# A second accumulator for the modulation sums, LayerNorm scaling between later splits, and attention's modulation one stage ahead

## The chip, the cores and the metric

The kernel runs on one core of a Trainium2 chip. The metric is the device time of one execution in microseconds: 3281.18 us, the median of three runs (3276.89 to 3293.57).

## What is computed

Two transformer blocks of two layers each, in float32, on 256 tokens of 1024 features. Each sublayer is steered by a modulation: a row of 9216 numbers, `silu(cond) @ w_mod + b_mod`, cut into shift, scale and gate for each of three sublayers. The first block has two streams (latent and context), each with a condition of its own.

```python
def modulation(cond, w_mod, b_mod):
    m = jax.nn.silu(cond) @ w_mod + b_mod
    return jnp.split(m[..., None, :], N_MOD, axis=-1)

def ffn_sublayer(x, shift, scale, gate, w_in, w_out, ln_g, ln_b):
    y = swiglu(modulate(x, shift, scale), w_in, w_out)
    return layer_norm(ALPHA * x + 0.5 * gate * y, ln_g, ln_b)
...
        x_lat = ffn_sublayer(x_lat, m_lat[0], m_lat[1], m_lat[2], ...)
        x_ctx = ffn_sublayer(x_ctx, m_ctx[0], m_ctx[1], m_ctx[2], ...)
        h_lat = modulate(x_lat, m_lat[3], m_lat[4])
        # gMLP in layer 0, grouped-query attention in layer 1, here y_lat, y_ctx
        x_lat = layer_norm(ALPHA * x_lat + m_lat[5] * y_lat, ln_g[i, 1], ln_b[i, 1])
        x_lat = ffn_sublayer(x_lat, m_lat[6], m_lat[7], m_lat[8], ...)
```

The second block has RMS norms, a mixer and one stream. The change doesn't touch its code.

## The kernel before

The program is a list of twelve stages, `subs`, numbered by `s["i"]`: 0 ffn, 1 gMLP, 2 ffn, 3 ffn, 4 attention, 5 ffn (first block), 6 to 11 the second block. Stages 0 to 3 work on both streams (512 tokens wide), stage 5 on one (256). Attention takes in both and gives out one. All five engines run one hand-written instruction stream each, and semaphores tie them together.

**Units.** Weights come in units of 1 MB, by SyncE, into two buffers `wraw`. ScalarE copies a unit to a rounded high half `wh` (L816), VectorE subtracts to get the low half `wl` (L1200, `split_next`), and TensorE makes three matmuls for each product (high-high, low-high, high-low). `split_next(u)` splits unit u + 1. The buffer of a unit is free to be split again when TensorE is done with the unit before, so a split stands on the way from one unit to the next but one.

**An ffn stage of two streams** has two groups, of 12 and of 10 units of `w_in`, each followed by an output phase of 6 or 5 units of `w_out`. A `w_in` unit is 48 matmuls (L2137) into a pair of PSUM banks. ScalarE takes silu of one half (L914), VectorE multiplies it with the other (L1580, "the product"), which frees the pair (`pair_free`), and GpSimd splits the result (L660, L661). The first two units of a stage are done stream by stream in `begin_two`, and `gate_rows` (L2067) follows them. Stage 0 has its gate rows after unit 2, since its gate is summed in the stage itself. Stage 5 has one group of 22 units.

**Modulation.** Each stage computes the modulation of the next one, `nxt`, in three sections (shift, scale, gate) of four pieces. A piece (`mod_unit`) is a 1 MB load into one of two buffers `mraw` and two accumulations for each condition (L1173, 128x1024) into `acc`. So a piece is four instructions with two streams and two with one. `acc` holds a sum that is still spread over the 128 partitions. For shift and scale TensorE sums it to columns, by matmuls with a vector of ones (`column` between the matmuls of a unit, L2056, or `columns` in one block, L2047). VectorE copies these out of PSUM (`mod_end`, L1193). For the gate `gate_rows` does the summing. There is one `acc`, so section 1 can begin only when section 0's columns are read. Tables give the unit at which each piece is summed (`TWO_MODS`), loaded (`TWO_LOADS`) and turned into columns (`TWO_COLUMNS`). They have one row for stage 0 (`True`) and one for stages 1 to 3. The order in VectorE's queue in unit i is: split, pieces, product, `mod_end`. Where the columns are in unit i, the first piece of a section comes after them (`late_mods`).

In attention (stage 4) all twelve pieces for stage 5 are spread by hand between the steps for keys, queries and heads, with `columns(nxt, 0, 7)` before unit 5 and `columns(nxt, 1, 6, 480)` at head 5.

**LayerNorm.** `layer_norm` leaves x without gain and bias. The next stage applies them in `scale_x` (L1316, four full-width operations for each stream), in its first output phase. `load_ln` on GpSimd's queue brings gain and bias to `lnp` (L675), in the stage before the one that uses them. VectorE lets it go on by `ln_used`.

**Queues.** SyncE issues all weight and modulation loads in one order. A piece's load waits until the piece two before it has been summed (`mod_used`), and all that stands behind it waits too. GpSimd issues the loads of gains.

Of the kernel before, what the change touches and what calls it, by code (L numbers as in the profile page):

```python
# [6 lines left out]
P = 128  # L7
# [38 lines left out]
ATT_LOADS = (1, 1, 5, 5, 7, 7, 8, 8, 9, 9, 9, 9)  # L46
# [132 lines left out]
def program(nc, ins, out, subs):  # L179
    u_end = subs[-1]["n_unit"] + dict(ffn=33, gmlp=36, attn=10, mix=16)[subs[-1]["kind"]]  # L180
    with ExitStack() as ctx:
# [247 lines left out]
        def early_mods(s, idx):  # L429

            return [(sec, q) for sec, q in two_mods(s, idx) if q or two_columns(s, idx) is None]

        def late_mods(s, idx):

            return [(sec, q) for sec, q in two_mods(s, idx) if not q and two_columns(s, idx) is not None]
# [44 lines left out]
        def _(sp):  # L480
# [83 lines left out]
            for s in subs:  # L564
# [15 lines left out]
                elif s["kind"] == "ffn":  # L580
                    m0 = 0
                    for g, n in enumerate(s["groups"]):

                        halves = lambda idx: [w_in[:, :, t, bass.ds(idx + m0, 1), :].rearrange("p k m c -> p k (m c)") for t in range(2)]
                        if two(s) and g == 0:
                            first_phase(s, n, halves, nxt, True)
                        else:
                            phase(n, 2 if g else 8, halves, None if g else nxt, by_column=True)
# [13 lines left out]
                elif s["kind"] == "attn":  # L602
# [8 lines left out]
                    for idx in range(10):  # L611
# [6 lines left out]
                        for n, at in enumerate(ATT_LOADS):  # L618
                            if at == idx:
                                load_mod(nxt, n // 4, n % 4, n // 4 * 4 + (12 * nxt["i"] + n % 4 + 1))  # L620
# [22 lines left out]
        def _(pool):  # L643
# [27 lines left out]
            def load_ln(s):  # L671

                pool.wait_ge(ln_used, s["i"])
# [39 lines left out]
            for s in subs:  # L713
# [30 lines left out]
                elif s["kind"] == "ffn":  # L744
                    m0 = 0
                    for g, n in enumerate(s["groups"]):
# [3 lines left out]
                        if g == 0 and s["i"] < B2 - 1:  # L750
                            load_ln(s)
# [18 lines left out]
                elif s["kind"] == "attn":  # L770
                    power(nrm1[:, 16:24], 8)
                    for u in range(4):
                        power(nrm1[:, 4 * u:4 * u + 4], 4)
                    load_ln(s)
# [32 lines left out]
        def _(act):  # L807
# [69 lines left out]
            for s in subs:  # L877
# [270 lines left out]
        def _(dve):  # L1148
# [11 lines left out]
            def mod_unit(s, sec, q):  # L1160
# [9 lines left out]
                for jj in range(2):  # L1170
                    for c in cs:
                        v = 2 if s["block"] == 2 else c
                        op = dve.scalar_tensor_tensor(out=acc[:, c], in0=mraw[:, q % 2, jj],  # L1173
                                                      scalar=svec[:, v, 2 * q + jj:2 * q + jj + 1],
                                                      in1=biasrow[:] if q == jj == 0 else acc[:, c],
# [326 lines left out]
            for s in subs:  # L1502
# [64 lines left out]
                elif s["kind"] == "ffn":  # L1567
# [3 lines left out]
                    for g, n in enumerate(s["groups"]):  # L1571
# [10 lines left out]
                        if two(s) and g == 0:  # L1582
                            for i in range(n):
# [7 lines left out]
                                for sec, q in early_mods(s, i):  # L1591
# [4 lines left out]
                                elif s["i"] == 0 and i == 2:  # L1596
# [1199 lines left out]
```

## Time and profile before

| | before |
|---|---|
| median of 3 runs | 3281.18 us (3276.89 to 3293.57) |
| profiled execution | 3288.56 us |
| its span | 3286.8 us |
| mean granted TensorE clock | 0.971 |
| instructions | 46905 |

The profile is of one execution. Where an instruction had to wait, its row has in brackets the idle time of the engine before it and who ended that. Stages in this execution, by the starts of their first units: 0 from about 50 us, 1 from 450, 2 from 920, 3 from 1330, 4 from 1735, 5 from 1903, the second block from 2112. The granted clock is a share of 2.4 GHz. A matmul's end is modelled, so neighbours overlap in the rows, and start-to-start times or windows are the safer measure.

### The profile page before, as it was taken

How to read it: one execution, taken by the hardware profiler on the slowest of the kernel's cores; microseconds unless marked ns; L12 is line 12 of the kernel's file. 1: busy time of each engine (PE TensorE's matmuls, PEld its weight loads, DVE VectorE, ACT ScalarE, POOL GpSimd, SP SyncE). 2: the span in 40 equal slices, each digit the busy share in tenths (PEclk: the TensorE clock that was granted, in tenths of full speed). 3: DMA queues.
4: the chain of work that ended last, by engine and by line, in shares of the span. 5: the costliest groups of instructions: out<-in, count | busy, mean ns of one | idle time of the engine just before them, and what ended most of it. 6: DMA issues, size and time to landing. Idle time of an engine off the chain costs nothing.

```text
span 3286.8 us, 46905 instructions
## 1 busy us (share of the span) xinstructions
PE 3116.7 (95%) x19332; PEld 2765.7 (84%) x19332; DVE 2028.1 (62%) x2134; ACT 986.5 (30%) x1027; POOL 688.1 (21%) x640
## 2 busy tenths in 40 slices
PE   8889999999998999989998899999989999999899
PEld 5668889978887888878887698899888999988899
DVE  4653357667366643765437777576687767667764
ACT  2111222212121112212113455333533334353433
POOL 1120110024112111121100011131371304228110
PEclk9989999999999999999999999999899999999999
DMA  7443335322235332443333477496546869754464
GB/s 250 151 156 94 98 90 181 128 90 77 91 114 167 133 97 90 125 153 133 90 118 118 165 218 246 161 269 229 179 167 179 269 207 263 244 183 151 149 184 155
DMA packets 501663, 522.73 MB, mean 159 GB/s; under 512 B 15732, under 2 KB 433830, under 8 KB 501478
## 3 DMA queue, kind: packets, MB, share of 16 engines
q1 hardware_dynamic: 498536, 513.76, 48.6%
q0 software_dynamic: 2944, 6.32, 0.9%
q8 instruction: 140, 2.29, 0.3%
q14 instruction: 43, 0.35, 0.0%
HBM read 518.97 MB, written 1.05 MB: 158 GB/s over the span
## 4 chain that ended last, share of the span: by engine, by line
PE 77%; DVE 13%; POOL 3%; issue 3%; ACT 3%; DMA 2%; SPq 0%; ACTq 0%; DVEq 0%; POOLq 0%
PE ps L2137 22%; PE ps L2311 15%; PE ps L2223 14%; PE ps L2335 7%; DVE acc L1173 5%; PE ps L2165 5%; DVE wl L1200 3%; PE ps L2202 2%; POOL wst L786 1%; PE ps L2181 1%; ACT wh L816 1%; PE ps L2047 1%; POOL lnp L792 1%; DMA mraw<-in_w_mod 1%; PE ps L2249 1%
## 5 line engine op out<-in xcount | busy, mean ns | idle before, releaser
L1200 DVE TENSOR_TENSOR wl<-wraw,wh 128x2048 fp32r<-128x2048 f32 x341 | 832.4, 2441 | 602.9 <-ACT wh L816 597.4
L816 ACT ACTIVATE wh<-wraw 128x2048 fp32r<-128x2048 f32 x341 | 652.7, 1914 | 952.1 <-PE ps L2223 406.7
L2137 PE MATMUL ps<-xh,wh 128*128 128x512 f32 (+1 forms) x1504 | 567.5, 377 | 7.1 <-DVE wl L1200 6.4
L2137 PE MATMUL ps<-xl,wh 128*128 128x512 f32 (+1 forms) x1504 | 554.7, 369 | 0.0
L2137 PE MATMUL ps<-xh,wl 128*128 128x512 f32 (+1 forms) x1504 | 553.9, 368 | 0.0
L1173 DVE SCALAR_TENSOR_TENSOR acc<-mraw,svec,acc 128x1024 f32<-128x1024 f32 x329 | 438.0, 1354 | 27.1 <-DMA mraw<-in_w_mod 11.0
L660 POOL CAST hh<-ht 128x256 f32 (+1 forms) x176 | 146.0, 830 | 1267.4 <-DVE ht L1580 934.1
L2311 PE MATMUL ps<-xh,wh 128*128 128x258 f32 x1408 | 403.4, 287 | 5.3 <-DVE xl L1398 4.4
L2311 PE MATMUL ps<-xh,wl 128*128 128x258 f32 x1408 | 399.5, 284 | 0.0
L2311 PE MATMUL ps<-xl,wh 128*128 128x258 f32 x1408 | 399.2, 284 | 0.0
L2137 PEld LDWEIGHTS ps<-xh,wh 128*128 128x128 f32 x1504 | 285.3, 190 | 54.9 <-issue 6.6
L2137 PEld LDWEIGHTS ps<-xl,wh 128*128 128x128 f32 x1504 | 284.8, 189 | 49.5
L2137 PEld LDWEIGHTS ps<-xh,wl 128*128 128x128 f32 x1504 | 285.3, 190 | 45.3 <-issue 0.7
L2311 PEld LDWEIGHTS ps<-xh,wh 128*128 128x128 f32 x1408 | 268.4, 191 | 10.2 <-DVE xl L1398 7.6
L2165 PE MATMUL ps<-wh,xh 128*128 128x256 f32 x832 | 247.7, 298 | 24.8 <-DVE wl L1200 24.8
L2311 PEld LDWEIGHTS ps<-xl,wh 128*128 128x128 f32 x1408 | 268.9, 191 | 0.0
L2311 PEld LDWEIGHTS ps<-xh,wl 128*128 128x128 f32 x1408 | 268.5, 191 | 0.0
L914 ACT ACTIVATE sg<-ps 128x512 f32<-128x512 f32 (+1 forms) x88 | 48.0, 546 | 653.4 <-PE ps L2137 620.0
L2165 PE MATMUL ps<-wl,xh 128*128 128x256 f32 x832 | 240.8, 289 | 0.0
L2165 PE MATMUL ps<-wh,xl 128*128 128x256 f32 x832 | 240.6, 289 | 0.0
L1580 DVE TENSOR_TENSOR ht<-ps,sg 128x512 f32<-128x512 f32 (+1 forms) x88 | 54.8, 623 | 291.7 <-ACT sg L914 291.7
L2223 PE MATMUL ps<-wh,hh 128*128 128x512 f32 x520 | 207.2, 398 | 10.1 <-DVE wl L1200 7.6
(423 smaller groups left out, 5658.0 us busy)
## 6 DMA issues: line engine op xcount, KB each, us to landing
wraw<-in_ffn_w_in SPq DMA_DIRECT2D x352, 512.0 KB, 5.1
wraw<-in_ffn_w_out SPq DMA_DIRECT2D x176, 512.0 KB, 4.2
mraw<-in_ada_w SPq DMA_DIRECT2D x72, 1024.0 KB, 7.0
mraw<-in_w_mod SPq DMA_DIRECT2D x64, 1024.0 KB, 6.8
wraw<-in_gmlp_w_in SPq DMA_DIRECT2D x48, 512.0 KB, 4.5
wraw<-in_mix_w_in SPq DMA_DIRECT2D x48, 512.0 KB, 4.7
wraw<-in_gmlp_w_out SPq DMA_DIRECT2D x24, 512.0 KB, 4.1
first_w<-in_w_mod SPq DMA_DIRECT2D x8, 1024.0 KB, 11.6
```

The lines of the kernel that those rows point to most:

```text
L660: steps.link(pool.tensor_copy(hh[:, where], ht[:, par, 0:width]))
L816: act.activation(wh[:, slot], wraw[:, slot], ACT.Copy).then_inc(whi_done, 1)
L914: act.activation(sg[:, pair, 0:W], ps[:, 2 * pair, 0:W], ACT.Silu).then_inc(sg_ready, 1)
L1173: op = dve.scalar_tensor_tensor(out=acc[:, c], in0=mraw[:, q % 2, jj], scalar=svec[:, v, 2 * q + jj:2 * q + jj + 1], in1=biasrow[:] if q = ...
L1200: dve.tensor_tensor(wl[:, slot], wraw[:, slot], wh[:, slot].bitcast(F32), ALU.subtract)\
L1580: dve.tensor_tensor(ht[:, pair, 0:W], ps[:, 2 * pair + 1, 0:W], sg[:, pair, 0:W], ALU.mult)\
L2137: m = pe.matmul(ps[:, bank, 0:width], a, b, start=k == p == 0, stop=k == KD - 1 and p == 2)
L2165: m = pe.matmul(to, a, b, start=k == p == 0, stop=k == KD - 1 and p == 2)
L2202: m = pe.matmul(ps[:, 2 * t + half], a, b, start=False, stop=i == kk == 1 and p == 2, skip_group_check=i == 0)
L2223: m = pe.matmul(ps[:, bank0 + 2 * t + half], a, b, start=start and kk == p == 0, stop=stop and kk == 1 and p == 2, skip_group_check=not st ...
L2311: m = pe.matmul(ps[:, 2 * pair + r, 0:XW], a, b, start=n == p == 0, stop=n == KD - 1 and p == 2)
L2335: m = pe.matmul(ps[:, j, 0:T], a, b, start=i == kk == p == 0, stop=i == KF // 2 - 1 and kk == 1 and p == 2, skip_group_check=i == 5)
```

## The change

- Section 1 of the modulation is summed into `lnp` in stages 0 to 3 (function `summed`), and `TWO_COLUMNS` moves the columns later: in stage 0 from units 6 and 9 to 7 and 10, in the others from 5 and 8 to 6 and 10. `early_mods` and `late_mods` go. All pieces of a unit come ahead of its product.
- `load_ln` moves into the stage that uses what it loads. It waits for section 1's columns.
- In two-stream stages `scale_x` is called for one stream at a time, after the second and the third split of the output phase and not before them all. In the gMLP the same.
- Stage 0's gate rows go from unit 2 to unit 3.
- Sections 0 and 1 for stage 5 leave attention for the second group of stage 3, two pieces in each of the units 2 to 5 (`NEXT_MODS`), with columns in units 5 and 7. They are summed in the two halves of `lnp`. Attention keeps section 2, at heads 1, 3, 5 and 6. For this, stage 3's second group is written out where it was a loop on VectorE, SyncE and TensorE.
- ScalarE's first group of stage 5 is written out too (`if g == 0`).

```diff
-ATT_LOADS = (1, 1, 5, 5, 7, 7, 8, 8, 9, 9, 9, 9)
+ATT_MODS, ATT_LOADS = (1, 3, 5, 6), (5, 5, 9, 9)
-TWO_MODS = {True: (3, 4, 4, 5, 6, 7, 8, 8, 9, 10, 11, 11), False: (2, 3, 3, 4, 5, 6, 7, 7, 8, 9, 10, 11)}
-TWO_LOADS = {True: (5, 6, 7, 7, 8, 9, 10, 10, 11, 11, 12, 12), False: (3, 4, 5, 6, 7, 8, 9, 9, 10, 11, 11, 12)}
-TWO_COLUMNS = {True: (6, 9), False: (5, 8)}
+TWO_MODS = {True: (4, 4, 5, 5, 6, 7, 7, 8, 9, 10, 10, 11), False: (2, 3, 3, 4, 5, 6, 7, 7, 8, 9, 10, 11)}
+TWO_LOADS = {True: (5, 6, 7, 7, 8, 9, 9, 10, 11, 11, 12, 12), False: (3, 4, 5, 6, 7, 8, 9, 9, 10, 11, 11, 12)}
+TWO_COLUMNS = {True: (7, 10), False: (6, 10)}
+NEXT_MODS, NEXT_LOADS, NEXT_COLUMNS = (2, 2, 3, 3, 4, 4, 5, 5), (3, 3, 5, 5, 6, 6, 7, 7), (5, 7)
...
+        def summed(s, sec, c):
+
+            if s["i"] == 5 and sec in (0, 1):
+                return lnp[:, sec]
+            return lnp[:, c] if 0 < s["i"] < 5 and sec == 1 else acc[:, c]
...
-            def load_ln(s):
-
-                pool.wait_ge(ln_used, s["i"])
+            def load_ln(at):
+
+                pool.wait_ge(ln_used, at["i"] - 1)
+                if at["i"] < 5:
+                    pool.wait_ge(mcol_done, sections(subs[5 if at["i"] == 4 else at["i"] + 1], 1) + 1)
+                s = subs[at["i"] - 1]
...
-                        if two(s) and g == 0:
+                        if g == 0:
                             for i in range(n):
-                                if i:
+                                if i or not two(s):
                                     split_next(u0 + i)
                                 evac(i, i % 2, 0)
...
-                                for sec, q in early_mods(s, i):
+                                for sec, q in two_mods(s, i):
                                     mod_unit(nxt, sec, q)
                                 evac(i, i % 2, 0)
...
-                                for sec, q in late_mods(s, i):
-                                    mod_unit(nxt, sec, q)
+                        elif s["i"] == 3:
+                            for i in range(n):
+                                split_next(u0 + i)
+                                for sec, q in ahead(s, i, NEXT_MODS):
+                                    mod_unit(subs[5], sec, q)
+                                evac(i, i % 2, 0)
+                                if ahead_columns(s, i) is not None:
+                                    mod_end(subs[5], ahead_columns(s, i))
...
-                        if g == 0:
+                        if one:
                             scale_x(s, s["post"])
-                            if unscaled(s):
-                                dve.sem_inc(ln_used, 1)
...
+                        if two(s) and g == 0:
+                            for i in range(n // 2 - 1):
+                                split_next(u0 + n + 1 + i)
+                                if 0 < i < 3:
+                                    scale_x(s, (i - 1,))
```

## Rows read from the trace of the kernel before

**Rows 1.** Page, section 1: busy us, share of the span, number of instructions
```profile
PE 3116.7 (95%) x19332; PEld 2765.7 (84%) x19332; DVE 2028.1 (62%) x2134; ACT 986.5 (30%) x1027; POOL 688.1 (21%) x640
```

**Rows 2.** Waits of TensorE: total us, times, longest
```profile
PE ps L2056 <- DVE acc L1173: 35.4, 8, 6.5
PE ps L2165 <- DVE wl L1200: 24.8, 9, 5.6
PE ps L2223 <- DVE wl L1200: 15.1, 4, 7.1
```

**Rows 3.** TensorE's timeline, stages 2 and 1: start, us, [idle before, releaser]
```profile
1004.32 0.38 PE L2056 MATMUL ps<-ones,acc 128*128 128x1 f32 x2 [2.25 <-DVE acc L1173]
...
1047.80 0.59 PE L2056 MATMUL ps<-ones,acc 128*128 128x1 f32 x2 [6.51 <-DVE acc L1173]
...
700.86 0.79 PE L2223 MATMUL ps<-wh,gm_h 128*128 128x512 f32 x1 [7.10 <-DVE wl L1200]
```

**Rows 4.** ScalarE's timeline: activations that end a unit, stages 0, 1, 2
```profile
103.87 0.60 ACT L914 ACTIVATE sg<-ps 128x512 f32<-128x512 f32 x1 [17.19 <-PE ps L2137]
...
150.50 0.60 ACT L914 ACTIVATE sg<-ps 128x512 f32<-128x512 f32 x1 [22.25 <-PE ps L2137]
...
196.04 0.60 ACT L914 ACTIVATE sg<-ps 128x512 f32<-128x512 f32 x1 [20.95 <-PE ps L2137]
...
550.75 1.09 ACT L932 ACTIVATE v<-ps 128x512 f32<-128x512 f32 x2 [13.08 <-PE ps L2165]
...
595.99 1.09 ACT L932 ACTIVATE v<-ps 128x512 f32<-128x512 f32 x2 [19.74 <-PE ps L2165]
...
1001.41 0.60 ACT L914 ACTIVATE sg<-ps 128x512 f32<-128x512 f32 x1 [8.59 <-PE ps L2137]
...
1018.43 0.60 ACT L914 ACTIVATE sg<-ps 128x512 f32<-128x512 f32 x1 [14.62 <-PE ps L2137]
...
1065.10 0.60 ACT L914 ACTIVATE sg<-ps 128x512 f32<-128x512 f32 x1 [22.07 <-PE ps L2137]
```

**Rows 5.** VectorE's timeline in stage 2, ahead of section 0's columns
```profile
981.87 3.28 DVE L1200 TENSOR_TENSOR wl<-wraw,wh 128x2048 fp32r<-128x2048 f32 x1 [1.11 <-ACT wh L816]
985.07 10.08 DVE L1173 SCALAR_TENSOR_TENSOR acc<-mraw,svec,acc 128x1024 f32<-128x1024 f32 x8
...
997.87 6.39 DVE L1173 SCALAR_TENSOR_TENSOR acc<-mraw,svec,acc 128x1024 f32<-128x1024 f32 x4
```

**Rows 6.** TensorE's timeline: the gate rows of stage 2
```profile
964.80 3.60 PE L2067 MATMUL ps<-acc,ones 128*128 128x512 f32 x8
```

**Rows 7.** Windows: stretch, its us, TensorE busy (instructions), PEclk, DMA share, GB/s
```profile
218.22:298.01 79.79, 71.30 (x288) 56.66 (x288) 0.94 0.35 116
682.32:737.32 55.00, 47.90 (x192) 37.75 (x192) 0.91 0.30 96
1098.10:1165.47 67.37, 67.36 (x288) 53.67 (x287) 1.00 0.34 110
...
700.00:704.00 4.00, 3.14 (x7) 0.50 0.98 258
```

**Rows 8.** Attention: window of L1173 on VectorE, and TensorE's column blocks
```profile
1753.93:1903.39 149.46, 30.77 (x24) 0.92 0.44 145
...
1808.48 3.57 PE L2047 MATMUL ps<-ones,acc 128*128 128x1 f32 x16 [4.69 <-DVE acc L1173]
...
1855.38 1.84 PE L2047 MATMUL ps<-ones,acc 128*128 128x1 f32 x16
```

**Rows 9.** Stage 5: a table load on ScalarE, and TensorE's waits for splits
```profile
1933.70 1.28 ACT L914 ACT_TABLE_LOAD   x1 [2.77 <-PE ps L2137]
...
PE ps L2137 <- DVE wl L1200: 4.9, 8, 1.2
```

**Rows 10.** DMA issues: queue, number, size, median us from issue to landing
```profile
mraw<-in_w_mod SPq DMA_DIRECT2D x64, 1024.0 KB, 6.8
...
lnp<-in_ln_b POOLq DMA_DIRECT2D x5, 512.0 KB, 5.8
```

More of the change, by code:

```diff
@@ L427, in two_columns, with ahead, ahead_columns @@
             return at.index(idx) if idx in at else None
[L429 to L435, printed above, removed]
+        def ahead(s, idx, table):
+            return [(n // 4, n % 4) for n, at in enumerate(table) if at == idx] if s["i"] == 3 else []
+        def ahead_columns(s, idx):
+            return NEXT_COLUMNS.index(idx) if s["i"] == 3 and idx in NEXT_COLUMNS else None
+        def summed(s, sec, c):
+            if s["i"] == 5 and sec in (0, 1):
+                return lnp[:, sec]
+            return lnp[:, c] if 0 < s["i"] < 5 and sec == 1 else acc[:, c]
         def two(s):
@@ L586, in _ @@
                             first_phase(s, n, halves, nxt, True)
+                        elif s["i"] == 3:
+                            for idx in range(n):
+                                load(unit[0] + idx, unit[0] + idx, halves(idx), True)
+                                for sec, q in ahead(s, idx, NEXT_LOADS):
+                                    load_mod(subs[5], sec, q, sec * 4 + (12 * 5 + q + 1))
+                            unit[0] += n
                         else:
@@ L1611, in _ @@
                         last = g == 1 and two(s)
-                        phase(n // 2 - (2 if last else 1), u0 + n + 1, 2)
+                        if two(s) and g == 0:
[3 more added lines that the diff above has]
+                                    scale_x(s, (i - 1,))
+                        else:
+                            phase(n // 2 - (2 if last else 1), u0 + n + 1, 2)
+                        if g == 0 and unscaled(s):
+                            dve.sem_inc(ln_used, 1)
                         u0 += n + n // 2
@@ L1699, in _ @@
                             split_next(u1 + i)
+                            if g == 0 and 0 < i < 3:
+                                scale_x(s, (i - 1,))
+                        if g == 0:
+                            dve.sem_inc(ln_used, 1)
                         u1 += n
@@ L1712, in stage, with unit @@
                         AV.wait(dve, name, 0)
-                    def unit(i, taken=()):
+                    def unit(i):
                         split_next(u0 + i)
-                        for n in taken:
-                            mod_unit(nxt, n // 4, n % 4)
                     def sums(name, squares, to):
@@ L2363, in _ @@
                                 m.then_inc(w_used, 1)
-                                if s["i"] == 0 and i == 2:
+                                if s["i"] == 0 and i == 3:
                                     gate_rows(s)
+                        elif s["i"] == 3:
+                            pe.wait_ge(y_half, s["n_half"] + g)
+                            for i in range(n):
+                                pe.wait_ge(wlo_done, u0 + i + 2)
+                                pe.wait_ge(pair_free, s["n_inq"] + m0 + i)
+                                sec = ahead_columns(s, i)
+                                for r in range(2):
+                                    m = features((u0 + i) % 2, 2 * ((s["n_inq"] + m0 + i) % 2) + r, r, slice(0, W), W, False,
+                                                 None if sec is None else lambda n: column(subs[5], sec, n))
+                                m.then_inc(w_used, 1)
                         else:
@@ L2531, in _ @@
                             scores(h + 2)
-                        if h == 5:
-                            AV.wait(pe, "lo_3", 0)
-                            columns(nxt, 1, 6, 480)
                         if h == 7:
```

58 lines of the change are left out of this document (23 added, 35 removed).

## The prediction

> **What bounds the kernel now.** I read the engine table of the page first. TensorE is busy for 3116.7 of 3286.8 us and VectorE for 2028.1 [rows 1]. So TensorE sets the time, and only two things can be won: the 170 us in which it stands, and work on it that is slower than it need be. The table of waits of TensorE says who makes it stand [rows 2]. First comes L2056 behind L1173, 35.4 us in 8 waits: `column` turns the summed modulation row into columns and finds the sum unfinished. Then come weight splits (L1200) that arrive late, 24.8 and 15.1 us. Single waits stand in TensorE's timeline [rows 3]: 2.25 us at 1004.32 and 6.51 at 1047.80 in stage 2, 7.10 at 700.86 in the gMLP.
>
> A wait costs more than itself. I measure that on ScalarE, whose activation waits for the end of each unit: its idle time grows by just what a unit is longer. A plain unit leaves it idle for 8.59 us. The unit with section 0's columns leaves 14.62, and the one with section 1's leaves 22.07 [rows 4]. The first is 6.03 over, of which the wait is 2.25 and the sixteen columns are the rest, 3.8 us. The second is 13.5 over: 6.51 wait, 3.8 columns, and 3.2 that neither explains. The windows of the output phases show what that is: the same 288 matmuls take 67.37 us at granted clock 1.00 in stage 2 and 79.79 at 0.94 in stage 0; 192 of them take 55.00 at 0.91 in the gMLP [rows 7]. After the gMLP's wait of 7.10 us the granted clock is 0.50, which is 1.2 GHz of 2.4, in the first 4 us [rows 7]. So I price each place by the lengthened unit or phase and not by the wait.
>
> **The columns and the second accumulator (stages 0 to 3).** Why is the sum late? VectorE's queue has a unit's split, its modulation pieces, then the product that frees PSUM. Two pieces are 10.08 us, so one is 5.0, and once 6.39 [rows 5]. Between them, from 995.15 to 997.87, stand a product and a split, 2.7 us; a split alone can take 3.28 [rows 5]. So a unit with two pieces is 12.8 us of VectorE or more, against 11.2 of TensorE (67.37 / 6) [rows 7]. In stage 2 the last piece of section 0 ends at 997.87 + 6.39 = 1004.26; TensorE was ready for it 2.25 us before 1004.32. The change puts those columns one unit (11 us) later, so the margin is 8 to 9 us. It also lets section 1 begin before they are read, in `lnp`, so the pieces are spread and not squeezed behind the columns. Section 1's columns go from unit 8 to unit 10. I walk the queue on from 1004.26 in stage 2 with these prices: TensorE ends unit 5 at 1012, unit 6 with the columns at 1027, and then a unit every 11. VectorE ends the product and the split of unit 6 at 1007, the first piece of section 1 at 1013, the second at 1023 (behind the product of unit 5 and a split), and the last two at 1043 (behind the product of unit 6 and a split). TensorE wants them at 1060, 17 us later, and every split ends 3 us or more ahead of its unit. In stage 0 the same walk leaves 5 us for section 0 and 12 for section 1. New pieces there are no more than before; only their order differs. What goes:
> - Stage 2: 14.62 − 8.59 − 3.8 = 2.2, and 22.07 − 8.59 − 3.8 = 9.7. Together 11.9. Stage 3 repeats the pattern to 0.3 us: 11.7.
> - gMLP (stage 1): of its two units with columns one has no wait and leaves 13.08, the other 19.74 [rows 4], so 6.7 goes.
> - Stage 0: 22.25 − 8.59 − 3.8 = 9.9, and 20.95 − 8.59 − 3.8 = 8.6. Its gate rows move behind unit 3. The unit that holds them leaves 17.19, 8.6 over; undisturbed gate rows cost 3.6 [rows 6], so 5.0 goes.
> - Stage 0's first output phase is 12.4 us longer than stage 2's [rows 7]. Its weights were late because SyncE's queue held the last modulation loads ahead of them, and these waited for pieces that stood behind the column wait. With the pieces earlier, the walk has the weights split about 2 us before TensorE asks. Gone: 12.4; what is late next is the last product, and it has the phase's two first tiles as cover.
>
> **LayerNorm scaling.** In the gMLP eight full-width operations stood in VectorE's queue ahead of two splits; TensorE waited 7.10 us [rows 3] and then ran slow. 192 matmuls at stage 2's pace are 44.9 us, and they took 55.0 [rows 7]: 10.1 goes. In the ffn stages there is no wait at this place, so the interleaving wins nothing there. Price: scaling now needs gain and bias that are loaded in the same stage, after the columns of section 1. The GpSimd queue issues that load behind its last split of hidden units. It lands after 5.8 us [rows 10]. Scaling starts after the second or third output unit is split, some 11 us on. Covered by one output unit; without that cover VectorE would stand with the next split behind it. The row speaks of loads that VectorE's splits ran beside as well.
>
> The Trainium skill, SBUF — State Buffer, section "SBUF: two separate sides", speaks against this move: a DMA issued by GpSimd needs it to write descriptors, and VectorE operations that hold the shared port keep it from that. [...]
>
> **Attention's modulation.** The stage has 24 accumulation instructions, 30.8 us of VectorE [rows 8], and VectorE is what its TensorE waits on. Sixteen of them (20.5 us), both column blocks and eight loads leave it; eight with two spaced loads stay. On TensorE itself goes: the 4.69 us wait, 3.57 and 1.84 us of columns, together 10.1 [rows 8]. That is the lower end. The upper is 20.5 + 5.4 = 25.9, if every instruction stood on the path. Following the query chain (sum, factor by GpSimd, turn, transposes, exponentials): the four pieces before the column wait hide partly behind waits for weights and for the factor, and from head 1 on TensorE's own work binds. I get 11 to 12.5 at each head, and take 12. The bounds I keep are 6 (another wait in its place) and 20.
> In stage 3's second group sixteen instructions, eight loads and two column blocks arrive. VectorE there: a split and a product, up to 4 us, and two one-stream pieces, four instructions of 30.77 / 24 us, 5.1: some 9 of 11.2 us. The splits stand ahead of the pieces. A 1 MB load lands in 6.8 us [rows 10], and a buffer turns round in 11.2. That is tight but ahead of need by one unit. Columns: eight in place of sixteen, 1.9 each time, −3.8.
>
> **Stage 5, a side effect.** ScalarE's loop over its 22 units is written out now. In the loop each turn of two units reloads the activation table twice, 1.28 us each [rows 9], between TensorE's end of a unit and the next split. TensorE waits 4.9 us there in 8 waits [rows 9]. Written out, one load is left. DMA is busy in this stage, so I take 3.5 (bounds 0 and 4.9). The wait at its output phase stays, since `one` keeps the scaling ahead of the split.
>
> The Trainium skill, ScalarE activation tables: per-element evaluation and per-set limits, section "Table sets in the compiler and the runtime", says that table loads are placed per block; that would be why the loop has them.
>
> **Sum.** Stage 0: 5.0 + 9.9 + 8.6 + 12.4 = 35.9. gMLP: 6.7 + 10.1 = 16.8. Stage 2: 11.9. Stage 3: 11.7 − 3.8 = 7.9. Attention 12. Stage 5 3.5. Together 88.0 us. The profiled execution took 3288.56 us (span 3286.8), the median of the runs is 3281.18, so 7.4 lower. 3288.6 − 88.0 = 3200.6; against the median 3193.2. I forecast 3193.
>
> **Rivals.** About 0.5% (16 us) is what a measurement of this kernel can tell from no change.
> 1. The moved pieces collide. In stage 3 each unit draws two 1 MB loads beside its weights, in one SyncE queue. If a load waits on a piece, the weights behind it come late, as in stage 0's output phase: that price is 12.4. Attention then gives 6. 88.0 − 12.4 − 6 = 69.6: 3212. For it: that very mechanism in rows 7. Against it: SyncE stands a unit ahead here. Chance 0.17.
> 2. Waits shrink but do not vanish. If VectorE is later than my walk by more than the 5 us of stage 0, TensorE still waits there and the slow stretches stay. Then stages 0 and 1 give half (26) and the others a third less (10): 52, 3229. For it: a piece of 5.0 us can take 6.39 [rows 5]. Chance 0.12.
> 3. The change does not do what it says: the queue of VectorE is as long as before, and TensorE waits for splits in place of sums. Left are attention and stage 5, 15: 3266. Against it: a unit with one piece needs 7.7 to 9.7 of 11.2 us. Chance 0.04.
> 4. Slower. The late LayerNorm load. If it lands later than about 14 us after its issue, VectorE stands in `scale_x`, the next split waits behind it, and TensorE too, in stages 1, 2 and 3. It decides against the whole change only from (88 + 16) / 3 = 35 us beyond that. At a landing of 50 us: 3 × 36 = 108 lost, 3301. The rows show 5.8. Chance 0.03.
> 5. More is won: attention gives 20 and stage 5 all of it, and stage 3's written-out group costs nothing for columns: 3181. Chance 0.06.
>
> **How the numbers follow.** The forecast has 0.58. The range takes in case 5 with its neighbourhood, case 1 and the faster part of case 2: 3174 to 3228. Faster by over 0.5% is everything but case 4 and most of case 3, which lies at the bound: 0.94. Within 0.5%: 0.03. Slower: 0.03.
>
> **What the new profile would show.** No wait of TensorE on the modulation sums in stages 0 to 3, and no idle time over about 13 us in front of an activation there (8.6 + 3.8). Stage 0's first output phase at 67 to 69 us; the gMLP's at 45. Attention's TensorE stretch, 149 us long, at 137 or so, with no L2047 work. Two or fewer table loads in stage 5. Eight-column blocks in stage 3's second group with no wait ahead of them. The forecast is wrong if waits for L1200 take the place of those for L1173, if VectorE waits for the gains in `scale_x`, or if weights come late from SyncE in stage 3.

## The result and the profile after

| | before | after |
|---|---|---|
| median (runs) | 3281.51 us (4) | 3187.11 us (4, 3177.8 to 3188.18) |
| ratio, 95% interval | | 0.9701 (0.9669 to 0.9732) |
| profiled execution, span | 3288.56, 3286.8 us | 3186.64, 3184.9 us |
| mean granted TensorE clock | 0.971 | 0.985 |
| instructions | 46905 | 46705 |

The forecast was 3193 us in a range of 3174 to 3228. The engine table of the page, against [rows 1]: TensorE is 37.0 us less busy, although it makes as many matmuls, and its idle time falls from 170 to 105 us.

```profile
PE   3079.7 (97%) x19332; PEld 2738.2 (86%) x19332; DVE 2031.3 (64%) x2134; ACT 958.2 (30%) x1006; POOL 693.3 (22%) x640
```

The table of TensorE's waits up to 2110 us (us in total, times, longest), against [rows 2], which count the whole program. Of the 24.8 us in their second row only 4.0 lie before 2110 us. The rest is in the second block, which the change leaves as it is. No wait on a modulation sum (now L1192) is left, and none on a split (L1219) is over 1.3 us. Attention's are the largest that remain of those that the change comes near. The first fence is of the kernel before, the second of the kernel after.

```profile
PE ps L2165 <- DVE wl L1200: 4.0, 3, 2.2
```
```profile
PE ps L2532 <- ACT ptb L1038: 6.9, 4, 3.3
PE ps L2491 <- DVE ql L1764: 6.8, 2, 4.9
...
PE ps L2185 <- DVE wl L1219: 1.8, 2, 0.9
PE ps L2243 <- DVE wl L1219: 1.7, 2, 1.3
```

VectorE's and TensorE's timelines in stage 2, against [rows 3, 5]. The sum of section 0 is ready at 939.19 + 6.39 = 945.6, and its columns begin at 954.20: 8.6 us to spare. Section 1's is ready at 983.9, its columns begin at 1001.88: 18 us.

```profile
939.19 6.39 DVE L1192 SCALAR_TENSOR_TENSOR acc<-mraw,svec,acc 128x1024 f32<-128x1024 f32 x4
...
973.83 10.09 DVE L1192 SCALAR_TENSOR_TENSOR lnp<-mraw,svec,lnp 128x1024 f32<-128x1024 f32 x8
...
954.20 0.28 PE L2076 MATMUL ps<-ones,acc 128*128 128x1 f32 x2
...
1001.88 0.28 PE L2076 MATMUL ps<-ones,lnp 128*128 128x1 f32 x2
```

ScalarE's activations that end those two units, against [rows 4]. Idle time was 14.62 and 22.07 us and is 12.1, a plain unit's 8.58 and the columns' 3.5.

```profile
953.71 0.60 ACT L932 ACTIVATE sg<-ps 128x512 f32<-128x512 f32 x1 [8.58 <-PE ps L2157]
968.20 0.60 ACT L932 ACTIVATE sg<-ps 128x512 f32<-128x512 f32 x1 [12.09 <-PE ps L2157]
...
1015.88 0.60 ACT L932 ACTIVATE sg<-ps 128x512 f32<-128x512 f32 x1 [12.08 <-PE ps L2157]
```

Windows of the first output phases of stage 0, the gMLP and stage 2, each from its first matmul, against [rows 7]. The columns here are the busy time of TensorE, its weight loads, VectorE, ScalarE and GpSimd, each with its number of instructions, then the granted clock, the DMA share and GB/s. All three run at clock 1.00. Stage 0's 79.79 us are 67.37, and the gMLP's 55.00 are 45.04.

```profile
189.99:257.36 67.37, 67.37 (x290) 54.04 (x289) 23.10 (x15) 11.97 (x7) 3.77 (x2) 1.00 0.33 104
633.18:678.22 45.04, 45.04 (x196) 36.24 (x195) 28.43 (x26) 6.68 (x4) 7.16 (x6) 1.00 0.36 117
1026.90:1094.27 67.37, 67.37 (x290) 54.03 (x289) 31.12 (x21) 11.96 (x7) 2.96 (x4) 1.00 0.36 110
```

I cut both profiled executions at the same events (first activation of a stage, first matmul of attention's end, second unit of stage 5's output phase) and compare the pieces:

| piece | forecast | gained |
|---|---|---|
| before stage 0's first activation (67.11 and 63.73) | 0 | 3.4 |
| stage 0 | 35.9 | 35.1 |
| gMLP | 16.8 | 20.2 |
| stage 2 | 11.9 | 12.1 |
| stage 3 | 7.9 | 9.4 |
| attention | 12 | 14.9 |
| stage 5 | 3.5 | 7.0 |
| second block | 0 | −0.1 |
| sum | 88.0 | 101.9 |

### The profile page after: what moved, and what is told of

The parts are those of the page before. It is cut to its first block, busy times and chain, and to the rows that moved or that the text cites. A ratio compares the mean times of both kernels' runs of the same rounds, so it can differ in the third digit from the quotient of the medians.

```text
span 3184.9 us, 46705 instructions
## 1 busy us (share of the span) xinstructions
PE 3079.7 (97%) x19332; PEld 2738.2 (86%) x19332; DVE 2031.3 (64%) x2134; ACT 958.2 (30%) x1006; POOL 693.3 (22%) x640
## 4 chain that ended last, share of the span: by engine, by line
PE 85%; DVE 8%; POOL 3%; ACT 2%; issue 1%; DMA 1%; SPq 0%; DVEq 0%; ACTq 0%; POOLq 0%
PE ps L2157 29%; PE ps L2331 15%; PE ps L2243 15%; PE ps L2355 8%; PE ps L2185 6%; PE ps L2222 2%; DVE wl L1219 2%; POOL wst L804 1%; PE ps L2201 1%; POOL lnp L810 1%; PE ps L2269 1%; PE ps L2065 1%; PE ps L2628 1%; ACT wh L834 1%; PE ps L2094 1%
## 5 line engine op out<-in xcount | busy, mean ns | idle before, releaser
L1219 DVE TENSOR_TENSOR wl<-wraw,wh 128x2048 fp32r<-128x2048 f32 x341 | 835.0, 2449 | 586.3 <-ACT wh L834 580.9
L1192 DVE SCALAR_TENSOR_TENSOR acc<-mraw,svec,acc 128x1024 f32<-128x1024 f32 x259 | 343.0, 1344 | 15.4 <-DMA mraw<-in_ada_w 10.2
L674 POOL TENSOR_TENSOR hl<-ht,hh 128x256 f32 (+1 forms) x176 | 219.2, 1246 | 29.2 <-POOL hh L673 29.2
```

What stands on the lines that cost most here:

```text
L674: pool.tensor_tensor(hl[:, where], ht[:, par, 0:width], hh[:, where].bitcast(F32), ALU.subtract)\
L1192: op = dve.scalar_tensor_tensor(out=to, in0=mraw[:, q % 2, jj], scalar=svec[:, v, 2 * q + jj:2 * q + jj + 1], in1=biasrow[:] if q == jj == ...
L1219: dve.tensor_tensor(wl[:, slot], wraw[:, slot], wh[:, slot].bitcast(F32), ALU.subtract)\
```

## Experiments

Each was timed against the kernel before on its own chip. Ratios are to be read beside the 0.9701 of the kernel after. Because a single execution scatters by several us, places are compared in the traces. How much it scatters shows behind stage 5's last silu: from there to the end, where only the faster version below changes anything, the 14 profiled executions take 1240 to 1250 us. Stage 0, the largest piece, has no experiment of its own: its 35.1 us rest on the comparison of the two traces.

### The later columns, or the second accumulator?

```diff
-TWO_COLUMNS = {True: (7, 10), False: (6, 10)}
+TWO_COLUMNS = {True: (7, 10), False: (5, 8)}
```

> The kernel after, with TWO_COLUMNS for stages 1 to 3 back at units 5 and 8; the second accumulator stays, and all pieces stay ahead of their product. It parts the two halves of that edit. Theory A, the later columns do the work: the sums stand as late as before, each of the six column units waits, about 2 us for section 0 and 6 us with a slow stretch for section 1, and the 30 us of stages 1 to 3 come back. Theory B, the single accumulator was the cause, since section 1 could only start behind section 0's columns: with the second one in place section 0 waits 2.2 us as before, section 1 no more than that, 13 us at most come back. Theory C, both are slack by now: 0.

Measured: 3219.30 us, ratio 0.9792 (0.9762 to 0.9822), 32 us slower than the kernel after by the medians and 30 by the ratios. In the trace the stretches from stage 0 to 2, from 2 to 3 and from 3 to 5 are each 10.1 to 10.4 us longer, 30.6 in all: theory A in its total. Its single waits were sized wrongly. TensorE's waits of that kernel:

```profile
PE ps L2076 <- DVE lnp L1192: 12.3, 3, 4.1
...
PE ps L2076 <- DVE acc L1192: 6.1, 3, 2.3
```

Section 1 waits 4.1 us in stages 2 and 3 and not 6.5, so the second accumulator alone does take waiting away, 2.4 us in each. But section 0's short waits are now followed by slow stretches: in stage 3 it waits 2.24 us, then the granted clock is 0.50 for 4 us, and the unit is 20.15 us long where before it was 17.00 with the same wait.

```profile
1357.00:1361.00 4.00, 4.00 (x13) 3.42 (x14) 4.00 (x3) 0.00 (x0) 3.16 (x2) 0.50 0.32 123
```

By the lengths of their units the columns gained 33.5 us in these stages (8.7, 12.5 and 12.3), and 30.6 go when the positions go back. The second accumulator seems to make room for the later positions, since section 1 need no longer start behind section 0's columns. That is argued and not shown: no run has the later columns with one accumulator.

### LayerNorm scaling alone

```diff
-                        if g == 0:
-                            scale_x(s, s["post"])
-                            if unscaled(s):
-                                dve.sem_inc(ln_used, 1)
-                        elif unscaled(nxt):
+                        if g and unscaled(nxt):
                             factors(nxt)
                         for i in range(n - g):
                             split_next(u1 + i)
+                            if g == 0 and 0 < i < 3:
+                                scale_x(s, (i - 1,))
+                        if g == 0:
+                            dve.sem_inc(ln_used, 1)
```

> The kernel before, with one part of the change: in the gMLP the LayerNorm scaling is called stream by stream behind the second and third split of the output phase. Theory A, the forecast's: the wait of 7.10 us goes, and with it the slow stretch behind it, so the 192 matmuls of that output phase take 45 us in place of 55.0: 10 us faster. Rival B: only the wait goes, the clock has fallen for another reason: 7 us. Rival C: the splits now stand behind the four operations of each stream and are late in turn: 0 to 3 us.

Measured: 3278.18 us (10 runs), ratio 0.9981 (0.9965 to 0.9997), so 1 to 11 us faster. The window of the output phase, from its first matmul to its end, is 45.04 us at clock 1.00, where [rows 7] has 55.00 at 0.91. That is theory A: 10.0 us, of which 7.10 were the wait. The median shows 7 of them; two column units of the same stage were 3.7 us longer in this execution, with nothing changed there.

```profile
684.86:729.90 45.04, 45.04 (x196) 36.24 (x195) 28.42 (x26) 6.69 (x4) 7.22 (x6) 1.00 0.37 117
```

### Does idling lower the clock?

`keep_going` is a helper that the kernel before has already: matmuls on constants whose result nobody reads.

```diff
                 if n == 0:
+                    if sec == 1:
+                        keep_going(7, 44)
                     pe.wait_ge(mod_used, sec * 4 + (12 * s["i"] + 6))
```

> The kernel before, with 44 matmuls of 128x128 on constants (0.117 us each, 5.15 us, from the row of 32 in 3.74 us) put ahead of TensorE's wait for section 1's sum in stages 0 to 3. The waits there are 6.51, 5.25, 6.51 and 6.50 us and TensorE has nothing else to do, so the useful work begins no earlier. Theory A, standing idle is what lowers the clock: the granted clock is 1.00 behind the wait and not 0.50, and each of the four units is 2.3 to 3.5 us shorter (8.85, 7.7, 10.0 and 9.7 over an undisturbed one, less the wait): 11 us faster than the kernel before. Rival B, the clock falls for another reason (the loads that come in just then, or the column matmuls): no change.

Measured: 3287.85 us, ratio 1.0004 (0.9993 to 1.0014). Not a verdict for B: I had mispriced the filler. In the trace each of its matmuls is two records. TensorE's row for it in stage 2:

```profile
1039.03 9.98 PE L2076 MATMUL ps<-ident,ones 128*128 128x128 f32 x88
```

The wait of 6.51 us has become 9.98 us of work, and still the unit ends as early as before (24.32 us after the one before it, against 24.47). In the gMLP and in stage 0 the filled unit is longer, by 2.1 and 0.7 us. What follows the filler runs at clock 1.00 in all four places, where before the same place has 0.50 (windows in stage 2, first of the kernel with the filler, second of the kernel before). The DMA share, the number before the last, speaks against incoming loads as the cause: it is 1.08 in the first window, at clock 1.00, and 0.00 in the second, at 0.50.

```profile
1050.00:1054.00 4.00, 4.00 (x23) 3.42 (x23) 0.00 (x0) 0.00 (x0) 0.37 (x1) 1.00 1.08 312
```
```profile
1047.80:1051.20 3.40, 3.40 (x10) 2.92 (x11) 2.75 (x2) 0.00 (x0) 2.51 (x2) 0.50 0.00 0
```

So I halved it (`keep_going(7, 22)`).

> The kernel before, with 22 filling matmuls ahead of the wait for section 1's sum, where the run with 44 had too many: there each is two records, 88 records took 9.98 us in stage 2, longer than the wait of 6.51, and the granted clock stayed 1.00. 22 take 5.0 us and fit in the wait. Theory A (idling lowers the clock, and the slow stretch costs useful time): clock 1.00 behind the wait, about 1.5 us of wait left, and the units of section 1 are 21 us in stages 2 and 3 in place of 24.47 and 24.23, in all four 9 to 11 us less. Theory B: the units keep their length, since what follows the wait is slow for another reason (columns that read a sum just written, loads coming in).

Measured: 3274.01 us, ratio 0.9956 (0.9939 to 0.9973), 9 to 20 us faster than the kernel before, with matmuls added that compute nothing. In stage 3 the filler takes 5.07 us, 1.59 of wait are left, the granted clock behind it is 1.00, and the unit is 21.26 us and not 24.23.

```profile
1450.38 0.38 PE L2058 MATMUL ps<-ones,acc 128*128 128x1 f32 x2 [1.59 <-DVE acc L1173]
```
```profile
1450.40:1454.40 4.00, 4.00 (x23) 3.48 (x24) 2.73 (x2) 0.00 (x0) 3.13 (x2) 1.00 0.02 5
```

Theory A holds where the wait was filled wholly: the slow stretch comes from standing idle, not from the loads or the columns. With half the filler it isn't sure at each place: in stages 0 and 2 of this run the clock behind the remaining 1.59 us was 0.63, and these units are only 0.5 and 1.6 us shorter. The four filled units are 7.0 us shorter together, less than the 9 to 11 expected, and section 0's units of the gMLP and stage 2, which have no filler, are 0.9 and 3.1 longer. Of the 11.1 us between the two profiled executions 7.6 lie behind stage 5's last silu, where nothing was changed. So the four runs are faster, but the traces account for only a part of it.

### Attention

```diff
-ATT_MODS, ATT_LOADS = (1, 3, 5, 6), (5, 5, 9, 9)
+ATT_LOADS = (1, 1, 5, 5, 7, 7, 8, 8, 9, 9, 9, 9)
...
                     queries(0)
+                    mod_unit(nxt, 0, 1)
...
-                        if h in ATT_MODS:
-                            mod_unit(nxt, 2, ATT_MODS.index(h))
+                        if h < 4:
+                            mod_unit(nxt, 1, h)
+                        elif h > 4:
+                            mod_unit(nxt, 2, h - 5)
```

with the remaining pieces and both column blocks back likewise, and none of it in stage 3.

> The kernel after, with the modulation of sections 0 and 1 for stage 5 back in attention (all twelve pieces, both column blocks, the old loads) and out of stage 3's second group. Theory A, the forecast's: attention is longer by its 12 (bounds 6 to 20), stage 3 shorter by 3.8 for eight columns twice: +8. Theory B, by the landmarks of the two traces: attention +14.9, stage 3 -3.8 (units 12.87 against 11.0), so +11. Rival: attention's gain came from entering it in a better state (no slow stretch, weights ahead) and not from the pieces: then it stays within 5 us of the kernel after.

Measured: 3197.18 us, ratio 0.9730 (0.9704 to 0.9755), 10 us slower than the kernel after. The windows from the first matmul of stage 3's last output phase to the first of stage 5, of the kernels before, after and this one (columns as in [rows 7], TensorE's, its weight loads', VectorE's, ScalarE's and GpSimd's busy time, then the clock):

```profile
1680.37:1903.39 223.02, 196.32 (x1089) 164.63 (x1088) 155.62 (x208) 75.30 (x103) 16.38 (x17) 0.95 0.41 136
```
```profile
1599.98:1808.36 208.38, 187.64 (x1057) 155.74 (x1056) 135.24 (x190) 75.20 (x103) 17.35 (x19) 0.98 0.33 107
```
```profile
1602.94:1828.71 225.77, 200.34 (x1089) 167.20 (x1088) 155.58 (x208) 75.30 (x103) 17.35 (x19) 0.93 0.40 136
```

The stage is 17.4 us longer and stage 3 is 2.7 shorter; the rest of the program, which is the same, was 2 us shorter in this execution. The pieces, then, are the cause. The stage is even 2.8 us longer than in the kernel before, at a clock of 0.93 and with 1.3 us less of recorded waits, so what the clock takes here differs by some 4 us between executions. The windows also divide the gain of the change, 14.6 us here: 5.4 are the columns (3.57 + 1.84), 6.1 are recorded waits (26.3 us before, 20.2 after), and 3.1 remain, which I put down to work at a clock of 0.98 in place of 0.95. No run parts that remainder from the rest. VectorE's 20.4 us less thus took only 6.1 us of waiting away: TensorE now waits for the queries (L2491) 6.8 us and for the exponentials as long as before.

### Stage 5

```diff
-                        if g == 0:
+                        if two(s) and g == 0:
                             for i in range(n):
-                                if i or not two(s):
+                                if i:
```

> The kernel after, with one thing undone: ScalarE's 22 units of stage 5 are a loop again. The forecast priced this edit at 3.5 us from TensorE's recorded waits (4.9 us), but by the same landmarks stage 5 is 7.0 us shorter after the change. Theory A: all 7.0 comes from the table loads, since each wait costs TensorE more than the trace records. Then this kernel is 7.0 us (0.22%) slower than the kernel after, 22 table loads are back, and the waits on the split of L1219 in stage 5 add up to about 5 us. Theory B: only the recorded waits come from the loop and the rest of the 7.0 from stage 5 starting in another state: then it is 3.5 to 5 us slower.

Measured: 3191.87 us, ratio 0.9708 (0.9673 to 0.9743), 5 us slower by the medians, which the runs alone can't tell from 3.5. The stretch from stage 5's first matmul to the second unit of its output phase can: 148.75 us, after 141.56, before 148.55. The whole 7.0 comes from this edit. How a recorded wait of 1.19 us costs more than 1.19 is seen in TensorE's timeline of the kernel before:

```profile
2031.56 0.28 PE L2137 MATMUL ps<-xh,wl 128*128 128x256 f32 x1
2031.68 0.28 PE L2137 MATMUL ps<-xl,wh 128*128 128x256 f32 x1
2033.15 0.39 PE L2137 MATMUL ps<-xh,wh 128*128 128x256 f32 x1 [1.19 <-DVE wl L1200]
2033.37 0.28 PE L2137 MATMUL ps<-xh,wl 128*128 128x256 f32 x1
```

Matmuls start every 0.12 us. The one behind the wait should have started at 2031.80 and starts at 2033.15, 1.35 late; the next follows after 0.22 and not 0.12. That is 0.27 us per wait on top. Eight recorded waits (4.9) make 7.1. In this run nine waits add up to 5.0 us, which with 0.27 on each is 7.4, and the stretch is 7.2 longer. The loads are in the table of groups for stage 5's 22 units, before and after (line, engine, operation, number, busy us and mean ns, idle):

```profile
L816 ACT ACT_TABLE_LOAD x11 | 14.1, 1283 | 2.2 <-DMA wraw<-in_ffn_w_in 1.6
L914 ACT ACT_TABLE_LOAD x11 | 14.1, 1283 | 30.5 <-PE ps L2137 30.5
```
```profile
L932 ACT ACT_TABLE_LOAD x1 | 1.3, 1283 | 0.0
```

A split's high half starts 1.77 us behind its activation with a load between (1927.24, 1929.01) and 0.28 without (1814.31, 1814.59). So a switch costs 1.5 us here, the load and 0.2. The Trainium skill, ScalarE: Activation LUTs, section "What ACT_TABLE_LOAD costs", adds a drain to each load and gives 2.66 us for every switch; this trace doesn't show the drain.

```profile
1927.24 0.38 ACT L914 ACTIVATE sg<-ps 128x256 f32<-128x256 f32 x1 [2.57 <-PE ps L2137]
1927.72 1.28 ACT L816 ACT_TABLE_LOAD   x1
1929.01 1.92 ACT L816 ACTIVATE wh<-wraw 128x2048 fp32r<-128x2048 f32 x1
```

Writing out the second groups of stages 0, 2 and 3 in the same way:

> The kernel after, with ScalarE's second groups of stages 0, 2 and 3 written out too, as its first groups and stage 5 are. It takes away 20 to 30 further table loads of 1.28 us. Theory A: in two-stream stages a unit of TensorE lasts 11 us and a split has several us to spare, so this is hidden: 0 us, though the loads go. Theory B: the units of those groups take 11.20 us and not 10.98 because ScalarE's loads delay something: then 0.22 x 9 units x 3 groups, 6 us faster.

Measured: 3183.06 us, ratio 0.9692 (0.9666 to 0.9718), no difference that the runs can tell. The units of those groups stay at 11.20 us. Theory A: with 11 us a unit the loads are covered.

### The rival that ends slower

```diff
                         if g == 0 and 0 < s["i"] < 5:
+                            pool.wait_ge(w_used, s["n_unit"] + 12 + 3)
                             load_ln(s)
```

> The kernel after, with GpSimd's load of the LayerNorm gains held back in stages 2 and 3 until TensorE is done with the third output unit, some 34 us later. It prices the rival that ends slower. VectorE reaches the scaling 23 us after the load's present issue; the load lands after 6. So VectorE stands about 17 us in the scaling. Theory A: two split buffers cover most of that; the next split must be done one unit (11 us) after it can begin, the load lands 6 us after that point, scaling takes 4.6 and the split 3.3, so TensorE waits 2 to 3 us in each of the two stages, 3 to 4 with its slow stretch: 5 to 8 us slower than the kernel after. Rival B, the price of the forecast's rival: every us of VectorE's wait is one of TensorE's: 17 in each stage, 34 us slower. Rival C: hidden wholly, 0.

Measured: 3188.87 us, ratio 0.9709 (0.9687 to 0.9732), within 2 us of the kernel after. VectorE and TensorE in stage 2 of it:

```profile
1069.79 4.63 DVE L1336 TENSOR_TENSOR x<-x,lnp 128x1024 f32<-128x1024 f32 x4 [12.84 <-DMA lnp<-in_ln_b]
...
1076.80 0.50 PE L2244 MATMUL ps<-wh,hh 128*128 128x512 f32 x1 [1.72 <-DVE wl L1220]
```

VectorE stands for 12.84 us and TensorE for 1.72: the two split buffers cover all but that. From the last silu ahead of the output phase to the first behind it the stretch is 1.8 us longer, in stage 3 1.6. Theory A in kind; its 5 to 8 us for both stages were too many for these 3.4. So a load that is issued 34 us later than now costs 1.8 us in a stage, and theory B's 17 are far off. A delay that outlasts the two buffers was not run. The stage as a whole was not even longer (389.6 us against 391.2), for the reason of the next run.

### Two paces of the same matmuls

In the second groups a unit of 48 matmuls lasts 11.20 or 10.99 us, at clock 1.00 both times.

```diff
                             if both:
                                 pe.wait_ge(y_half, s["n_half"] + g)
+                                small(s["n_inq"] + m0, 1 if s["i"] == 0 else 8)
```

where `small` waits for `pair_free`, as the unit behind it does, and makes so many matmuls of 128x1 on constants.

> The kernel after, with small matmuls (128x1 on constants) ahead of the second group's first unit: one in stage 0, eight in stage 2, none in stage 3. In the two traces a unit of the same 48 matmuls lasts either 10.99 or 11.20 us for a whole group, and changes from one to the other behind a unit with column matmuls. Theory A, a short matmul shifts TensorE's pipeline into the faster pace: the units of these groups last 10.99 us, 9 x 0.21 = 1.9 us for each of two stages, 3 to 4 us in all. Theory B, the pace comes from something else (weights that come in, ScalarE, VectorE): units stay at 11.20 and the time within 1 us.

Measured: 3185.72 us, ratio 0.9694 (0.9666 to 0.9722). ScalarE's idle time ahead of an activation, in stage 0's second group, of the kernel after and of this one:

```profile
279.86 0.60 ACT L932 ACTIVATE sg<-ps 128x512 f32<-128x512 f32 x1 [8.80 <-PE ps L2157]
```
```profile
279.95 0.60 ACT L932 ACTIVATE sg<-ps 128x512 f32<-128x512 f32 x1 [8.58 <-PE ps L2163]
```

One small matmul puts all nine units that follow at 10.99 us, eight do the same in stage 2, and stage 3, without any, stays at 11.20: theory A. The nine units take 98.89 us and not 100.79. The run's time doesn't show it: from stage 0's last silu to the gMLP's first activation it was 1.3 us longer in exchange, which leaves 0.5 of stage 0's 1.9, and stage 2 is 1.9 us shorter. The delayed load did the same by accident: behind its 1.72 us of waiting stage 2's second group runs at 10.99, and behind 1.54 us stage 3's.

### A faster version

One small matmul ahead of all three groups, ScalarE's second groups written out, and stage 5's scaling behind the third split of its output phase:

```diff
-                        if one:
-                            scale_x(s, s["post"])
...
-                        if two(s) and g == 0:
+                        if one or g == 0:
                             for i in range(n // 2 - 1):
                                 split_next(u0 + n + 1 + i)
-                                if 0 < i < 3:
+                                if one and i == 1:
+                                    scale_x(s, s["post"])
+                                elif not one and 0 < i < 3:
                                     scale_x(s, (i - 1,))
```

> The kernel after, with three additions: one 128x1 matmul ahead of the second group of stages 0, 2 and 3, which puts units of 11.20 us at 10.99; ScalarE's second groups written out; stage 5's LayerNorm scaling behind the third split of its output phase and not ahead of the second. By the traces: 1.9 us for each of stages 0 and 2, 1.0 in stage 3 (its first five units), the 1.3 us wait in stage 5's output phase gone: 6 us faster than the kernel after, if the output phases behind the faster units keep their length; 3 us if they give half of it back, as stage 0's did with one small matmul (85.15 against 83.82).

Measured: 3180.96 us, ratio 0.9674 (0.9661 to 0.9687). TensorE has no wait in stage 5's output phase. To compare on one chip, both again:

> The combined version again. If its gain is real, it is 4 to 7 us (0.12 to 0.22%) faster than the kernel after on the same chip; if the first difference of medians (6 us) was scatter between chips, the two are within 2 us.

> The kernel after itself, beside the combined version on one chip, so that the two are compared with the same runs of the kernel before. Each theory expects a ratio of 0.970 for it. Its start (first silu at 63.7 or at 67 us) and the pace of the gMLP's first units have taken two values in the traces so far, whatever the kernel, so single executions may differ by 3 to 8 us.

Measured: 3178.56 us, ratio 0.9667 (0.9645 to 0.9688), and the kernel after 3187.68, ratio 0.9704 (0.9683 to 0.9725). So the combined version is faster by about 9 us of medians, a little more than its traces add up to (1.9 + 1.9 + 1.0 + 1.3 and the 0.27 of the wait, 6.4). The two intervals just overlap, but both ratios have the same runs of the kernel before under them, and all five times of the combined version (3171.0 to 3182.66) lie below all five of the kernel after (3184.21 to 3191.55). On the first chip, by the ratios, it was 9 us ahead of the kernel after as first measured. Which of the three additions brings how much was not timed.

## Why the prediction was right, point by point

- **Columns.** The walk along VectorE's queue gave margins of 8 to 9 and 17 us in stage 2 and 5 us for section 0 in stage 0. The trace has 8.6 and 18, and 4.6 (sum ready at 123.7, columns at 128.27). Only section 1 in stage 0 had 8 us and not 12 (156.7, 164.96). Every priced wait went, and pricing by the lengthened unit was the step that carried the forecast: by waits alone, stage 2 would have given 8.8 and not 12.1. The run with the whole filler shows why.
- **Stage 0.** 35.9 against 35.1. The four terms came in whole: the output phase lost its 12.4 us, and the three units 5.2, 10.2 and 8.9. The second group fell into the slower pace (11.20 for 10.99, nine times, 2 us). The trace of before did hint at it: there stages 2 and 3, whose output phases have no wait, already ran their second groups at 11.20, and only stage 0, with waits of 5.97 and 2.51 us in that phase, at 10.99.
- **gMLP.** The scaling term was exact (10.1, measured 10.0 with that edit alone). The columns term was too small, 6.7 against 8.7: I had taken the unit with 13.08 us of idle time as free of waiting, and it isn't. Its wait is the eighth of those in [rows 2]:

```profile
535.87 0.38 PE L2056 MATMUL ps<-ones,acc 128*128 128x1 f32 x2 [0.77 <-DVE acc L1173]
```

The unit went from 15.96 to 14.92 us, and the other one was compared with it, so both came out 1.0 short. The last 1.5 goes with the pace of the first units (10.88 for 11.31), which varies between executions of the same code.
- **Stage 3.** 7.9 against 9.4: the column units there lost 12.3 and not 11.7, and behind the new column blocks the last units run at 10.98.
- **Attention.** 12 against 14.9. The mechanism was right, and waits and columns came to 11.5. What is missing is a remainder of about 3 us that I put down to the clock: I had not counted what the waits do to the work behind them, though I had done so in every other stage.
- **Stage 5.** The term that was mis-sized most, 3.5 against 7.0, outside its own bounds (0 to 4.9). The upper bound was the sum of recorded waits, and that isn't one: 0.27 us come on top of each. The bound should have been the loads on the path, or the lengthened pair of units, as elsewhere.
- **The start and the execution.** 3.4 us of the 101.9 come before the change does anything. In 14 profiled executions the first activation stands at 63.4 to 64.0 us in eight and at 66.5 to 67.3 in six, with the old and the new kernel in both groups. The traces show what parts them: behind a wait of 2.71 us at about 45 us the granted clock is 0.50 in all of the six and 1.00 in all of the eight (windows of the kernels before and after).

```profile
45.46:49.46 4.00, 4.00 (x19) 4.00 (x20) 2.74 (x3) 4.00 (x5) 0.40 (x1) 0.50 0.77 179
```
```profile
44.79:48.79 4.00, 4.00 (x35) 4.00 (x36) 2.74 (x3) 4.00 (x5) 0.39 (x1) 1.00 0.95 225
```

The profiled execution of before was 7 us above its median, that of after at its median. So the runs gained 94.4, with the forecast's 88.0 about 6 us short. Part of that closeness is luck. The forecast was counted from a median of three runs, 3281.18, and later medians of the same kernel, of 7 to 19 runs, are 3284.25 to 3286.40. On the chip where both kernels were timed again the gain is 98.7 us, and the 88.0 are 11 short.
- **The rivals.** No collision in stage 3 (no wait there), no waits for splits in place of sums, and the late load, even forced by 34 us, costs 1.8 us a stage: its price up to that delay, every us of VectorE's wait as one of TensorE's, was too high by the cover of two buffers. The loads of gain and bias themselves, issued beside VectorE's splits, land after 3.9 and 5.6 us in the median, where they took 4.0 and 5.8 before. The fifth case, more won at attention and stage 5, named the right places.

Open: what sets the pace, and when a wait of 1.6 to 2.3 us lowers the clock and when not.

## What to carry to other kernels

Price a wait by what it does to the length of the unit or phase around it, not by its recorded length: here a 6.5 us wait cost 9.9, one of 7.1 cost 10.0, and one of 0.6 cost 0.9. When a producer is late by a little, move the consumer by one unit first; a second buffer may be what gives the room to do it. A loop on ScalarE that alternates a function with copies can reload its table twice a turn; where units are short, write it out.

## What the hardware showed that was not expected

- The granted clock fell to 0.50 behind each wait of 5.3 to 7.1 us that I looked at, and behind waits of 1.6 to 2.3 us sometimes: with a wait of 2.25 us it was 1.00 in stage 2 of the kernel before and 0.50 in the same place of the kernel with half the filler. Filler matmuls over the whole wait kept it at 1.00 in four places of four, and the kernel was no faster. When they filled all but 1.6 us of it they kept it there in two places of four, and the kernel was 9 to 20 us faster. Not every long wait is followed by the slow clock: the first of the program, 8.1 us for a load and with no work of TensorE's ahead of it, was followed by 1.00 in the kernel before.
- The same 48 matmuls of 128x512 take 10.99 or 11.20 us at clock 1.00, for whole groups of units. The shorter one followed a single matmul of 128x1, a column block, and waits of 1.5 and 1.7 us.
- The start of the program takes 3 us more or less by the clock behind one wait of 2.71 us: 0.50 in six executions of 14, 1.00 in eight.
- A wait of TensorE cost 0.27 us more than its record says, at clock 1.00 (start to start, stage 5). Two waits of the run with the late load agree: with 1.72 and 1.54 us on record, the 288 matmuls around them took 1.99 and 1.81 us longer from first start to last (66.96 us without).
- Switching ScalarE's table cost 1.5 us, of which 1.28 is the load.
